# First blocks of three layers begun with one token group alone, and the feed forward's u and g computed with features on partitions

## The reference

```
x = layer_norm(ALPHA * x + attention_mixer(x, ...), ln_gain[0], ln_bias[0])    # border 1
x = layer_norm(ALPHA * x + retention_mixer(x, ...), ln_gain[1], ln_bias[1])    # border 2
h = rms_norm_2(x, norm_attn) * (1 + scale1) + shift1
x = x + gate1 * (attention of h) @ w_out                                       # border 3
h = rms_norm_2(x, norm_ffn) * (1 + scale2) + shift2
x = x + gate2 * conv_ffn(h, w_up, conv_w, conv_b, w_down)

def conv_ffn(h, w_up, conv_w, conv_b, w_down):
    u, g = jnp.split(h @ w_up, 2, axis=-1)          # 2048 -> 5632 and 5632
    u = lax.conv_general_dilated(                   # width 3 over tokens, one filter per feature
        u, conv_w[:, None, :], window_strides=(1,), padding=((CONV_WIDTH - 1, 0),),
        dimension_numbers=('NWC', 'WIO', 'NWC'), feature_group_count=D_FF) + conv_b
    return (jax.nn.silu(u) * g) @ w_down
```

## Time and profile before

| | us |
|---|---|
| time, median of 3 runs | 2290.98 (2285.35 to 2291.1) |
| profiled execution, its own time | 2291.69 |
| its span | 2290.0 |
| PE, DVE, ACT, POOL busy | 2230.9, 1702.5, 995.1, 141.6 |
| border 1: last output product, first product of the next block | 401.06, 408.54 |
| border 2: first product of the next block | 1187.58 |
| border 3: last output product, first product of the next block | 1527.57, 1536.75 |
| feed forward, from its first product to the last | 1536.75 to 2280.3 |

### The profile page before, as it was taken

One profiled execution on the slowest core, in us unless ns is written; L12 is line 12 of the kernel. 1 busy time (PEld: TensorE's weight loads), 2 busy tenths in 40 slices (PEclk: granted clock), 3 DMA queues, 4 the chain that ended last, 5 costly groups with the idle time before them and its releaser, 6 DMA issues.

```text
span 2290.0 us, 28816 instructions
## 1 busy us (share of the span) xinstructions
PE 2230.9 (97%) x10634; PEld 1842.1 (80%) x10634; DVE 1702.5 (74%) x1908; ACT 995.1 (43%) x1017; POOL 141.6 (6%) x202
## 2 busy tenths in 40 slices
PE   7999999999999999999999999999999999999998
PEld 6878887787888888888787778778888888888886
DVE  6788887988868878688795666985665667665567
ACT  4443433534434334343343455454444444444444
POOL 2110010010000000000011001000000000000000
PEclk9999999999999999999999999999999999999999
DMA  7877775697777777787646546455555556555653
GB/s 266 284 258 257 255 263 209 211 330 267 273 263 269 271 262 279 248 277 267 245 152 211 177 139 172 141 167 183 186 190 193 183 183 195 189 183 183 192 190 132
DMA packets 260288, 503.57 MB, mean 220 GB/s; under 512 B 14705, under 2 KB 68385, under 8 KB 259328
## 3 DMA queue, kind: packets, MB, share of 16 engines
q1 hardware_dynamic: 228480, 381.73, 50.2%
q0 software_dynamic: 31376, 119.80, 15.0%
q10 hardware_dynamic: 368, 1.18, 0.1%
HBM read 498.90 MB, written 3.69 MB: 219 GB/s over the span
## 4 chain that ended last, share of the span: by engine, by line
PE 84%; DVE 7%; DMA 3%; issue 2%; ACT 2%; SPq 0%; POOL 0%; DVEq 0%; POOLq 0%; ACTq 0%
PE pair_t L422 26%; PE pair_t L424 25%; PE pair_t L423 25%; PE turn L563 1%; DMA raw<-in_attn_w_in_dram 1%; DVE w_lo L408 1%; ACT w_hi L403 1%; PE sc L832 1%; DVE m_acc L1084 1%; PE sc L824 1%; DMA raw<-in_ret_w_in_dram 1%; PE sc L1695 1%; PE sc L682 1%; DMA raw<-in_ret_w_out_dram 0%; DVE x_mid L529 0%
## 5 line engine op out<-in xcount | busy, mean ns | idle before, releaser
L408 DVE TENSOR_TENSOR w_lo<-raw,w_hi 128x2048 fp32r<-128x2048 f32 (+1 forms) x364 | 815.6, 2243 | 461.0 <-ACT w_hi L403 456.4
L403 ACT ACTIVATE w_hi<-raw 128x2048 fp32r<-128x2048 f32 (+1 forms) x367 | 688.8, 1879 | 1029.1 <-DMA raw<-in_ret_w_in_dram 331.3
L422 PE MATMUL pair_t<-w_hi,x_hi 128*128 128x512 f32 (+1 forms) x2080 | 814.1, 391 | 18.0 <-DVE w_lo L408 12.4
L424 PE MATMUL pair_t<-w_hi,x_lo 128*128 128x512 f32 (+1 forms) x2080 | 799.6, 384 | 0.0
L423 PE MATMUL pair_t<-w_lo,x_hi 128*128 128x512 f32 (+1 forms) x2080 | 799.0, 384 | 0.0
L422 PEld LDWEIGHTS pair_t<-w_hi,x_hi 128*128 128x128 f32 x2080 | 393.6, 189 | 102.4 <-DVE w_lo L408 14.5
L424 PEld LDWEIGHTS pair_t<-w_hi,x_lo 128*128 128x128 f32 x2080 | 393.3, 189 | 78.0
L423 PEld LDWEIGHTS pair_t<-w_lo,x_hi 128*128 128x128 f32 x2080 | 393.9, 189 | 72.9 <-issue 0.2
L1084 DVE SCALAR_TENSOR_TENSOR m_acc<-m_raw,csilu,m_acc 128x1024 f32<-128x1024 f32 x180 | 230.8, 1282 | 8.0 <-DMA m_raw<-in_w_mod_dram 4.6
L422 PE MATMUL pair_t<-w_hi,f_hh 128*128 128x512 f32 x352 | 138.2, 393 | 1.5 <-DVE f_y L2278 1.0
L424 PE MATMUL pair_t<-w_hi,f_hl 128*128 128x512 f32 x352 | 137.0, 389 | 0.0
(11 more groups left out here) (364 smaller groups left out, 2143.5 us busy)
## 6 DMA issues: line engine op xcount, KB each, us to landing
m_raw<-in_w_mod_dram POOLq DMA_DIRECT2D x96, 1024.0 KB, 6.4
raw<-in_ret_w_in_dram SPq DMA_DIRECT2D x192, 512.0 KB, 4.5
raw<-in_w_up_dram SPq DMA_DIRECT2D x176, 512.0 KB, 4.2
raw<-in_w_down_dram SPq DMA_DIRECT2D x88, 512.0 KB, 4.4
raw<-in_attn_w_in_dram SPq DMA_DIRECT2D x64, 512.0 KB, 4.7
raw<-in_ret_w_out_dram SPq DMA_DIRECT2D x64, 512.0 KB, 4.8
raw<-in_w_in_dram SPq DMA_DIRECT2D x56, 512.0 KB, 4.6
raw<-in_attn_w_out_dram SPq DMA_DIRECT2D x32, 512.0 KB, 5.1
```

The costliest lines, as they stand in the source:

```text
L403: act.activation(chunk(w_hi, c, width), chunk(raw, c, width), ACT.Copy).then_inc(sem("hi"), 1)
L408: v.tensor_tensor(chunk(w_lo, c, width), chunk(raw, c, width), chunk(w_hi, c, width).bitcast(F32), ALU.subtract).then_inc(sem("lo"), 1)
L422: pe.matmul(to, xh, wh, start=start, stop=False)
L424: return pe.matmul(to, xl, wh, start=False, stop=stop)
```

## The change

**Three borders.** The transposes and the first block run by token group. `turn_token` turns four 128x128 tiles of one token (a quarter q); `project_by_token` takes the half chunks (q, t) in the order of the table FIRST. The affines of the quarters 0 and 2 are DVE's (`mid_token`, four of 128x128), those of 1 and 3 ACT's (`hi_token`, L580 in the new file), and z is normalized and scaled by quarters too. The fills go from 12 to none at border 1, from 54 to 44 at border 2, from 15 to none at border 3. At border 1 the first quarter is turned inside the last output block; behind border 2, m_part's matmul comes after the block as before.

**Feed forward.** For g of the first group and u and g of the ten others, the weights stand and the tokens move (`project_tiles`): for each tile of 128x128, w_lo takes x_hi of both tokens (256 columns), w_hi takes x_hi and x_lo, which now lie beside each other (512 columns), in one PSUM bank. ACT copies the half that belongs to x_lo, DVE adds the halves (f_us, f_gs). `load_tiles` brings 128 columns of all 2048 rows for a chunk, where `load` brings 512 columns of 512 rows.

**Attention.** The transpose of a_k moves to the tenth step of the gate's product, those of the first two heads' probabilities from between the output's chunks to the end of the gate. Some semaphores are merged.

```
+        def load_tiles(sp, b, w, first):
+            for c in range(CH):
+                sp.wait_ge(sem("products"), CH * b + c - CH + 1)
+                for h in range(2):
+                    to = raw[:, c, 2 * h:2 * h + 2, :].rearrange("p a (b n) -> p (a b) n", n=P)
+                    src = w[:, KC // 2 * h:KC // 2 * (h + 1), bass.ds(first + c * P, P)]
                     sp.dma_start(to, src).then_inc(sem(f"chunk_in{c}"), 16)
...
+        ring = [turn[0], turn[1], sc[0], sc[1]]
+        def project_tiles(pe, b, free, after=None):
+            for c in range(CH):
+                free(c)
+                pe.wait_ge(sem("lo"), CH * b + c + 1)
+                for k in range(KC):
+                    cols_of = slice(k % 4 * P, (k % 4 + 1) * P)
+                    wh, wl = w_hi[:, c, k // 4, cols_of], w_lo[:, c, k // 4, cols_of]
+                    if k:
+                        pe.matmul(ring[c][:, 0:T], wl, x_hi[:, k, :], start=False, stop=False)
+                    mm = pe.matmul(gview(ring[c][:, :], 2), wh, x_hl[:, :, k, :], start=k == 0, stop=k == KC - 1)
+                    if k == 0:
+                        pe.matmul(ring[c][:, 0:T], wl, x_hi[:, k, :], start=False, stop=False)
+                mm.then_inc(sem("products"), 1)
...
+        FIRST = {1: [(0, 0), (1, 0), (0, 1), (1, 1), (2, 0), (2, 1), (3, 0), (3, 1)],
+                 2: [(0, 0), (1, 0), (2, 0), (0, 1), (1, 1), (2, 1), (3, 0), (3, 1)],
+                 3: [(0, 0), (1, 0), (0, 1), (1, 1), (2, 0), (2, 1), (3, 0), (3, 1)]}
+        def turn_token(pe, n, t, groups):
+            src = z if n == 1 else z_s
+            for q in groups:
+                token_ready(pe, n, t, q)
+                if t == 1 and q < 2:
+                    pe.wait_ge(sem("turn_hi"), group_count(n, 0, q))
+                for k in range(CH):
+                    mm = pe.transpose(group_bank(t, q)[:, k * P:(k + 1) * P],
+                                      src[:, t, (CH * q + k) * P:(CH * q + k + 1) * P], ident[:, :])
+                mm.then_inc(sem("turned"), 1)
+        def project_by_token(pe, b, banks, n, between):
+            for c, t in FIRST[n]:
+                if t == 0:
+                    pe.wait_ge(sem("lo"), CH * b + c + 1)
+                pe.wait_ge(sem("turn_lo"), group_count(n, t, c))
+                for k in range(CH):
+                    kk = CH * c + k
+                    mm = product(pe, banks[t][:, :], x_hi[:, kk, t * P:(t + 1) * P], x_lo[:, kk, t * P:(t + 1) * P],
+                                 c, k, CB, kk == 0, kk == KC - 1)
...
+        def hi_token(act, n, t, q, gain, bias):
+            if q % 2:
+                act.wait_ge(sem("turned"), turned_count(n, t, q))
+                for k in range(CH):
+                    kk = CH * q + k
+                    ins = act.activation(x_mid[:, kk, t * P:(t + 1) * P], group_bank(t, q)[:, k * P:(k + 1) * P],
+                                         ACT.Identity, bias=bias[:, kk:kk + 1], scale=gain[:, kk:kk + 1])
+                ins.then_inc(sem("turn_mid_a"), 1)
+            act.wait_ge(sem("turn_mid_a" if q % 2 else "turn_mid"), middle_count(n, t, q))
...
                 elif c == 3:
                     scores(2)
                     scores(3)
-
-            def between(c):
-
-                if c == 1:
                     turn_probs(0)
                     turn_probs(1)
-                elif c == 2:
+
+            def between(c):
+
+                if c == 2:
...
             for k in range(4):
-                if k % 2 == 0:
-                    act.wait_ge(sem("f_u_turned"), 2 * f + k // 2 + 1)
-                ins = act.activation(f_c[:, k, :], turn[k // 2][:, k % 2 * T:(k % 2 + 1) * T], ACT.Identity,
+                ins = act.activation(f_c[:, k, :], f_us[:, k, :], ACT.Identity,
                                      bias=f_par[:, k, 3:4], scale=f_par[:, k, 2:3])
...
-            for j in range(2):
-                load(sp, f_block(0, j), f_blocks[j](0))
+            load(sp, f_block(0, 0), cols(w_f, 0))
+            load_tiles(sp, f_block(0, 1), w_f, FF)
             with sp.Fori(1, FG) as f:
-                for j in range(2):
-                    load(sp, f_block(f, j), f_blocks[j](f))
+                load_tiles(sp, f_block(f, 0), w_f, f * CB)
+                load_tiles(sp, f_block(f, 1), w_f, FF + f * CB)
                 load(sp, f_block(f, 2), out_rows(w_f_out, f - 1))
```

More of the change, by code:

```diff
@@ L1946, in pe_feed_forward, with turn_second @@
-            project(pe, f_block(f, 0), pair[0], before=u_before,
-                    pairs=(lambda: pe.wait_ge(sem("turn_lo"), 26)) if first else None,
-                    slot=turn_later(pe, 3, lambda j: scaled_copy(pe, 2, j), True)
-                    if first else None)
-            def g_before(c):
-                if c == 0 and not first:
-                    pe.wait_ge(sem("f_g"), f)
-                    pe.wait_ge(sem("f_scaled"), 2 + 4 * (f - 1))
+            def turn_second(c, t, k):
+                if (c, t, k) == (0, 0, 3):
+                    turn_token(pe, 3, 1, range(2))
+                elif (c, t, k) == (1, 0, 1):
+                    turn_token(pe, 3, 1, range(2, CH))
@@ L2585, in vec_feed_forward @@
             S_()
-            if not first:
+            if first:
+                S_(3)
+            else:
                 low(f, f_hh, f_hl)
-            S_(3)
-            S_()
+                for h in range(2):
+                    whole(f_us, f_ub, h, "f_ub", 2 * (f - 1) + h + 1, "f_us")
+                    S_()
             v.wait_ge(sem("f_par"), f + 1)
+            v.wait_ge(sem("f_us"), 2 * f + 2)
             v.wait_ge(sem("f_tap"), f + 1)
```

550 lines of the change are left out of this document (316 added, 234 removed).

## The result

The changed kernel takes 2310.06 us (median of 4 runs, 2308.08 to 2312.04) where the kernel before takes 2291.04 (2285.35 to 2292.69): ratio 1.0082, 95% interval 1.0067 to 1.0097. It is slower by some 19 us, and outside of the forecast range. The profiled run after has a span of 2308.5 us, 18.5 more than that of before.

What follows compares the result with a forecast made beforehand. TensorE, busy 97%, was taken as the bound: instruction counts in the feed forward, ACT and DVE chains at the borders. 2291.7 - 10.8 (feed forward) - 2.5 (attention) + 3 + 6 + 4 (borders) = 2291.4; forecast 2291, range 2275 to 2302.

Steps and rivals of the forecast that it cites:

- A tile block at 22.19 us: Feed forward: a block of 64 wide and 64 narrow products takes 22.19 us for 21.76, +9.0 us for 21.
- What was removed: Feed forward: 21 groups of eight transposes fall away, 0.88 us each, -18.6 us; the f_g wait goes too, -1.2.
- The 2.5 ns: Feed forward: the skill's gap per matmul instead of the trace's 13.3 ns; would put the sum near 2284 us.
- The attention, -2.5: Repeated heads: moved transposes fill 2.4 us of the a_sg waits, a_k's move gives 0.1; taken -2.5 us.
- Border 1, +3: Border 1: first product 3.4 us earlier, but chunk 3 is split later and the block ends at 434.6 for 432.1; +3.
- The walk: Border 1: hand-made timing through ACT's and DVE's queues; first product 405.1, chunk 3's split ending at 429.2.
- Border 2, +6: Border 2: first product at 1184.3 for 1187.6, but chunk 3's split and m_part late, +5 to +6.7 us; taken +6.
- Border 3, +4: Border 3: three ACT scalings in succession, no gain at the first product, block ends +2 to +4 us later; taken +4.
- B (neutral borders): Rival: the borders are neutral or better as the walk binds only in part; 2278.4 us, chance 0.36.
- C (the clock): Rival: PE's waits before chunk 3 at the borders bring half-clock stretches; up to 2302.7 us, chance 0.20.
- D (short runs): Rival: feed-forward weight loads in short runs become the bound, up to +59 us; chance 0.04, mostly small amounts.
- the rounding of chunk 3 behind every x_hi: All three borders: it stands last in ACT's queue, with half the affines now ahead; argued for the forecast case, chance 0.40.

Runs made afterwards that it cites:

- ff_groupedx: ff_alone with the tile products grouped by two: two of 256 columns, then two of 512; 2283.37 us, ratio 0.9961.
- after_contig: The changed kernel with x_hi and x_lo of each feature tile side by side, so the 512 moving columns are one run; 2307.85 us, ratio 1.0064.
- before_nofillx: The kernel before without the 12 fills of border 1 and the 15 of border 3; 2296.47 us, ratio 1.0012.
- ff_alone: The kernel before with only the changed kernel's feed forward and the merged semaphores, borders and attention as before; 2287.91 us, ratio 0.9985.
- new_borders_fixed_fill: new_borders_fixed with fill matmuls ahead of the first products of borders 1 (6) and 3 (15); 2282.19 us, ratio 0.9948.
- new_borders_fixed: The changed kernel with chunk 3 handled earlier, border 3 reordered, m_part's matmul later and 256-column products in a row; 2283.72 us, ratio 0.9956.

## Why the prediction was wrong

The sum said 2291.4, and the profiled run took 2310.2, 18.8 more. By the table's stretches, measured less forecast: feed forward +6.5, border 3 +4.5, border 1 +2.9, border 2 +0.4, attention -0.9, and three places that the sum had at nothing: the last output of the attention +2.1, that of the retention +2.3, the start +0.9.

- **A tile block at 22.19 us: the step that failed first.** The measured term is 22.59, so 21 blocks add 17.4 us and not 9.0. I took the 256-column step from a row where such products follow each other, and the 512-column one likewise; mixed, a pair takes 0.353 us and not 0.347. Half of the mixing removed brought 0.45 us in two blocks (ff_groupedx), so it is the order of widths and not the layout (after_contig) or the DMA. What was removed was sized well: the feed forward with g moved by -4.3, so it is worth 21.7 for my 19.8. A turn of the loop before, 67.10 us with 288 products of 0.2267, leaves 0.90 us for a group of eight transposes (0.88 in the sum), and PE's waits for f_y fell by 0.7, which I had not counted.
- **The 2.5 ns.** The sum by the Trainium skill (TensorE: Matmul & The Clock Gate, "Back-to-back issue gap") would have been 7.3 us lower still, further from the result. The trace's 13.3 ns was right for products of one width: with the widths in rows of 16 a pair takes 347.9 ns where 346.7 were taken.
- **The attention, -2.5.** Measured -3.4 in its stretch; the a_sg waits are gone as forecast. Its last output took 2.1 more: the four transposes of border 1's first quarter stand in it (some 0.5), and the rest is half clock behind the wait for a_ol, which the profiles of before_nofillx and ff_alone, with the old attention, have too.
- **Border 1, +3: mis-sized by 2.9.** The walk itself held: it had PE through with (2,1) near 424.7 and the split of chunk 3 ended at 429.2; the profile has 424.57 plus a product and 429.40. The first product came at 404.40 (405.1 walked) and the last output product at 400.75 (401.06 before), since the half clock and the inserted transposes used up what the attention had won. What failed is the end: it was reckoned at full clock, and the two half chunks took 8.4 us and not 5.4. Four affines on ACT took 1.49 and not 1.3. Measured -3.8 and +9.8, together +5.9.
- **Border 2, +6.** Measured -2.9 and +9.3, +6.4. m_part came 4.05 us late, behind the split of chunk 3, as walked.
- **Border 3, +4: mis-sized.** Measured +1.2 and +7.3, +8.5. I let the three scalings follow each other at 0.63 us; in ACT's queue x_hi of quarter 0 stands ahead of the first, the squares of token 1 and the affine of quarter 1 ahead of the others, and PE waited 2.87 us twice. I had read the names in the order, and not counted what stood between them.
- **The rivals.** B (neutral borders) is out: the borders cost 21 us in the stretches and 22.7 between two timed kernels. C (the clock) was the true mechanism for a part: half-clock stretches behind border 1 (two), 2 (one) and 3 (two), 7.2 us lost there for 1.4 before. Its time of 2302.7, with every size at its upper end, is still 7 us short of the result, by the tile blocks (6.5 in the feed forward). Not all of it is net: where the next group is late anyway, the slower clock costs nothing (new_borders_fixed_fill). D (short runs) is out.
- **Two us by chance.** The wait of 2.2 for z in the last output of the retention is in this profile, and not in that of after_contig, nor in most others (1.16 in before_nofillx, 1.47 in new_borders_fixed).
- **What the chances said.** Two of the reasons for "slower" were in the working, at 0.24 with the others: the clock, and the rounding of chunk 3 behind every x_hi. The widths and the order of the scalings were not. The error was in adding terms taken at their middle, when three of them (clock, ACT's queue, widths) had their surprises on one side.

Open: whether each border's new form alone, repaired, is worth anything. They were only timed together, and the split by stretches above is from one profile of each kernel. No run moved DVE's work in the block behind border 1, so that its queue is what costs the retention 2.9 of the 3.9 us is read from the trace and not tested.

## What to carry to other kernels

When work is handed from a busy engine to an idle one, look at what stands behind it in that engine's queue: here the affines went to ACT, busy for 43%, and the rounding of the next weights, which already stood last in the row, came at 425.06 instead of 421.40, beside a gap of 3.7 us in which it would have fitted. Beginning a block earlier is worth nothing if its last input is not earlier too, and a wait ahead of it may be paid again in clock. Price a mix of instruction shapes by a row in which they are mixed.

## What the runs showed of the hardware

- Products of 256 and 512 columns in turn take longer than the sum of both in rows of their own: two blocks of 64 and 64 took 45.17 us in turn, 44.72 by twos, 44.53 by sixteens, and 128 times the two steps of 0.2267 and 0.1200 are 44.38.
- TensorE's clock went to its lower level (1.2 of 2.4 GHz; products of 512 columns 0.43 us apart for 0.227) behind idle times as short as 1.7 us, at places that changed from profile to profile. Behind the wait of 2.14 us for a_ol it was full in those of before and ff_groupedx and half in the twelve others; behind the wait of 1.7 us for z at border 1 it was half in that of the changed kernel and full in that of after_contig.
- The time of one kernel goes with the mean granted clock of its run. Of the 24 and 31 runs of the kernel before in the first two groups, those at 0.998 took 2285 to 2287 us, those at 0.993 2292 to 2302 (correlation of time and clock -0.79 and -0.91). So much of the spread of 2285 to 2302 us is the clock; what moves it from run to run, no run here shows.
